# A tenth 2 MB place for experts' weights, a smaller ring for POOL's DMAs, three gather buffers instead of four

## What is computed

```python
def first_block(x, ...):
    h = rms_norm(x, norm_gain); proj = h @ w_in
    # attention over 31 compressed blocks, selected blocks and a window, all with
    # a shared bias by distance (rel_bias, 32 buckets); then the recurrence
    ...
    return x + m @ w_out

def second_block(x, ...):
    ...
    x = x + gate1 * (merged @ w_out)
    h2 = rmsnorm(x, norm2_w) * (1.0 + scale2) + shift2
    return x + gate2 * hierarchical_moe(h2, w_rg, b_rg, w_re, b_re, w_gate, w_up, w_down)

def hierarchical_moe(h, ...):       # top group, then 2 of its 8 experts for each token
    ...
    for e in range(N_EXPERTS):      # w_gate[e], w_up[e]: 1024 x 256, w_down[e]: 256 x 1024
        act = silu(hf @ w_gate[e]) * (hf @ w_up[e])
        y = y + combine[:, e:e + 1] * (act @ w_down[e])
```

## Time and profile before

| | |
|---|---|
| median of 3 runs | 1302.39 us (1296.23 to 1302.81) |
| the profiled execution, its own time | 1295.32 us |
| its span, first to last instruction | 1293.5 us |
| TensorE busy | 1220.6 us, 94% of the span |
| VectorE, ScalarE, POOL busy | 559.5, 307.6, 249.5 us |
| TensorE's mean granted clock | 0.983 of full speed |
| HBM read, written | 205.20 MB, 14.75 MB |
| share of the chain that ended last: TensorE, SP's queue, VectorE, DMA | 75%, 10%, 6%, 4% |

### The profile page before, as it was taken

The page is one execution under the profiler, slowest core; times in us unless marked ns, Lnnn a source line. Parts: engine busy times, 40 slices in busy tenths (PEclk is TensorE's granted clock), DMA queues, the critical chain, the costliest instruction groups (busy, mean ns, idle before and its releaser), DMA issues.

```text
span 1293.5 us, 13577 instructions
## 1 busy us (share of the span) xinstructions
PE 1220.6 (94%) x5056; PEld 692.7 (54%) x5056; DVE 559.5 (43%) x1432; ACT 307.6 (24%) x725; POOL 249.5 (19%) x221
## 2 busy tenths in 40 slices
PE   6999999999989999999999989999999999988885
PEld 3555444454544444488884445866674564433343
DVE  2214383477648751217992367522222442222221
ACT  4223644433310101124113245400000221111110
POOL 6100022354510000062420030302300021211100
PEclk9999999999999999999999999999999999998988
DMA  9625104223166514222223010302229489999995
GB/s 331 117 74 130 65 30 101 82 90 139 65 226 212 167 62 147 97 83 100 96 69 127 3 64 28 100 9 65 66 98 394 175 334 398 409 400 412 411 408 197
DMA packets 94935, 212.85 MB, mean 165 GB/s; under 512 B 20109, under 2 KB 54301, under 8 KB 83047
## 3 DMA queue, kind: packets, MB, share of 16 engines
q1 hardware_dynamic: 81344, 190.51, 39.8%
q0 software_dynamic: 10320, 18.80, 5.8%
q10 hardware_dynamic: 3200, 2.61, 0.6%
HBM read 205.20 MB, written 14.75 MB: 170 GB/s over the span
## 4 chain that ended last, share of the span: by engine, by line
PE 75%; SPq 10%; DVE 6%; DMA 4%; ACT 3%; issue 2%; ACTq 0%; POOL 0%; POOLq 0%; DVEq 0%
SPq L2825 8%; PE PS L2287 7%; PE PS L998 6%; PE PS L641 5%; PE PS L1415 4%; PE PS L2350 4%; PE PS L1495 4%; PE PS L1678 4%; PE PS L1680 4%; PE PS L2458 3%; PE PS L2957 3%; PE PS L1424 2%; PE PS L1724 2%; DMA AN<-in_w_down 2%; PE PS L1736 2%; PE PS L713 2%
## 5 line engine op out<-in xcount | busy, mean ns | idle before, releaser
L998 PE MATMUL PS<-HT,W 128*128 128x512 f32 x256 | 124.7, 610 | 1.8 <-ACT AN L1162 1.7
L1260 POOL TENSOR_SCALAR AN<-AN,SM 128x128 f32<-128x128 f32 (+3 forms) x64 | 72.5, 1140 | 197.2 <-DVE SM L1352 197.2
L1283 DVE SCALAR_TENSOR_TENSOR AN<-AN,COLA 128x256 f32<-128x256 f32 x168 | 85.9, 511 | 5.4 <-DMA AN<-in_w_ada 0.5
L2957 PE MATMUL PS<-AN,HT 128*64 128x512 f32 x192 | 61.6, 632 | 10.6 <-DMA X<-in_w_up 6.4
L641 PE MATMUL PS<-W,HT 128*128 128x512 f32 (+1 forms) x192 | 70.9, 531 | 0.0
L998 PEld LDWEIGHTS PS<-HT,W 128*128 128x128 f32 x256 | 44.4, 193 | 39.0 <-issue 35.4
L3042 DVE TENSOR_TENSOR HT<-HT,PS 128x256 f32<-128x256 f32 x16 | 6.7, 421 | 131.6 <-ACT HT L3017 131.6
L1415 PE MATMUL PS<-HT,W 128*128 128x512 f32 x128 | 58.1, 599 | 0.0
L2458 PE MATMUL PS<-W,AN 128*128 128x512 f32 x128 | 57.6, 597 | 0.0
L1242 ACT ACTIVATE AN<-PS,SM 128x128 f32<-128x128 f32 (+3 forms) x64 | 33.6, 525 | 93.9 <-DVE SM L1331 93.6
L2350 PE MATMUL PS<-AN,W 128*128 128x512 f32 x128 | 55.7, 593 | 0.1
(11 more groups left out here) (519 smaller groups left out, 2281.6 us busy)
## 6 DMA issues: line engine op xcount, KB each, us to landing
W<-in_w_in SPq DMA_DIRECT2D x14, 2048.0 KB, 9.0
W<-in_w_down SPq DMA_DIRECT2D x20, 1024.0 KB, 27.0
AN<-in_w_gate SPq DMA_DIRECT2D x17, 1024.0 KB, 26.9
AN<-in_w_up SPq DMA_DIRECT2D x17, 1024.0 KB, 28.8
AN<-in_w_ada SPq DMA_DIRECT2D x16, 1024.0 KB, 5.3
AN<-in_w_down SPq DMA_DIRECT2D x12, 1024.0 KB
W<-in_w_gate SPq DMA_DIRECT2D x10, 1024.0 KB, 24.4
W<-in_w_up SPq DMA_DIRECT2D x10, 1024.0 KB, 26.6
```

Source lines behind the costliest of these rows:

```text
L998: t = pe.matmul(u.ap, w[:, c, tile(m)], hT[:, c, :], start=c == 0, stop=c == 7)
L1260: pool.tensor_scalar(PU[u % 5][:, 0:n], PU[u % 5][:, 0:n], RSUM[:, u:u + 1], None, ALU.mult).then_inc(*sc_pool.up(u))
L1283: dve.scalar_tensor_tensor(out=a, in0=wt[:, c, :], scalar=ca["c2"][:, c:c + 1], in1=a, op0=ALU.mult, op1=ALU.add).then_inc(*ada_dve.up(p, c))
L2957: t = pe.matmul(u.ap[r, :].rearrange("p (n f) -> p n f", n=2), XGT[e % 2][:, c, r], w_gu(3 * e + half)[:, c], start=c == 0, stop=c == 7)
```

## The change

There are four parts. POOL's scratch of descriptors shrinks from 16384 to 4096 bytes a partition. The 12288 bytes (3072 numbers a partition) that this frees stand ahead of the area `AN`, and with the first 1024 numbers of `AN`, row 0 of `XN`, they make a tenth place. The gathers have three buffers, rows 3, 1 and 2 of `XN`, since row 0 is now part of that place. The four reads of `BCT` move from POOL's queue to SP's, with a semaphore of their own.

SP's order changes with it: the first half of load 9 goes out ahead of all other experts' loads and waits for nothing; the second half stands behind the second half of load 7 and waits for row 0 of `XN` to be written out and read by `pe_first_rows`. With NE = 10, it is loads 10 and 11 whose first halves wait for `first_pe`.

```diff
-    AN = sbuf("AN", AR)
+    ANX = sbuf("AN", 3072 + AR)
+    AN = ANX[:, 3072:3072 + AR]
...
-    XG = [XN[:, i, :] for i in range(4)]
+    XG = [XN[:, i, :] for i in (3, 1, 2)]
...
-    WE = [AN[:, a:a + 4096] for a in (6160, 10256, 18448)] + W[0:3] + [AN[:, 14352:18448], X, W[3]]
+    WE = [AN[:, a:a + 4096] for a in (6160, 10256, 18448)] + W[0:3] + [AN[:, 14352:18448], X, W[3], ANX[:, 0:4096]]
...
+    def sp_line(sp, ws):
+        ws.wait_ge(*line_out.at())
         for r in range(4):
-            pool.dma_start(BCT[31 * r:31 * r + 31],
-                           bass.AP(scr.tensor, 2048 * r, [[16, 31], [4 * 2048, 2], [1, 512]])).then_inc(*line_back.up())
+            sp.dma_start(BCT[31 * r:31 * r + 31],
+                         bass.AP(scr.tensor, 2048 * r, [[16, 31], [4 * 2048, 2], [1, 512]])).then_inc(*rows_back.up())
...
     def pe_bias(pe, wp):
...
             pe.matmul(u.ap, flip, REV[:, j * 512:(j + 1) * 512], start=True, stop=True).then_inc(*u.filled)
+        wp.wait_ge(*rows_back.at())
...
     def act_headnorm(act, wa):
...
+        wa.wait_ge(*rows_back.at())
...
-            act.dma_start(xnd[tile(i), :], XN[:, i, :]).then_inc(*xn_out.up())
+            act.dma_start(xnd[tile(i), :], XN[:, i, :]).then_inc(*xn_out[i].up())
...
     def wait_place(w, m, half=1):
...
-        else:
+        elif m == 8:
             w.wait_ge(*B.use("wo2", 3, 1).full)
+        elif half:
+            w.wait_ge(*xn_out[0].at())
+            w.wait_ge(*row_pe.at(0))
...
     def sp_expert(sp, ws, m, halves=(0, 1)):
         e, kind = divmod(m, 3)
         for n in halves:
-            wait_place(ws, m, n)
+            if m in (NE, NE + 1) and n == 0:
+                ws.wait_ge(*first_pe.at())
+            else:
+                wait_place(ws, m, n)
...
     def sp_expert_parted(sp, ws, e):
...
-                if m - NE in (0, 1) and n == 0:
-                    ws.wait_ge(*first_pe.at())
-                else:
-                    wait_place(ws, m)
+                wait_place(ws, m)
...
     def sp_experts(sp, ws):
+        sp_expert(sp, ws, 9, (0,))
         for m in range(6):
             sp_expert(sp, ws, m)
...
         sp_expert(sp, ws, 7, (1,))
-        for e in range(NE // 3, NP):
-            if e in (NE // 3, NP - 2, NP - 1):
+        sp_expert(sp, ws, 9, (1,))
+        for n in range(2):
+            sp_expert(sp, ws, 10, (n,))
+            sp_expert(sp, ws, 11, (n,))
+        for e in range(4, NP):
+            if e in (NP - 2, NP - 1):
...
     def pool_gather(pool, wg, e):
...
-        wg.wait_ge(*(row_pe.at(e) if e in (1, 2) else B.use("xg", max(e - 4, 0), 1).full))
+        wg.wait_ge(*(row_pe.at(e) if e in (1, 2) else B.use("xg", e - 3, 1).full))
         pool.indirect_dma_start(
-            out=XG[e % 4], ...
+            out=XG[e % 3], ...
...
     def sync_program(sp):
...
         sp_kvq(sp, ws)
+        sp_line(sp, ws)
         sp_cmp(sp, ws)
...
-    nc = _bacc.Bacc("TRN2", target_bir_lowering=False, num_devices=1)
+    nc = _bacc.Bacc("TRN2", target_bir_lowering=False, num_devices=1, dynamic_dma_scratch_size=4096)
```

More of the change, by code:

```diff
@@ L407, in build @@
         "consts_in", "gain_in", "line_in", "rows_in", "w2c_in", "small_in", "bd_in", "bars_in", "wr_in", "more_constants_in", step=16)
-    line_out, line_back, xn_out = sig("line_out", "line_back", "xn_out", step=16)
+    line_out, line_back, rows_back = sig("line_out", "line_back", "compressed_rows_back", step=16)
+    xn_out = sig(*[f"xn{i}_out" for i in range(NT)], step=16)
     x_spilled = sig(*[f"x{i}_spilled" for i in range(NT)], step=16)
@@ L418, in build @@
     stage_in = sig(*[f"stage{i}_in" for i in range(4)], step=16)
-    xg_in = sig(*[f"xg{i}_in" for i in range(4)], step=16)
+    xg_in = sig(*[f"xg{i}_in" for i in range(3)], step=16)
     yo_out = sig(*[f"yo{i}_out" for i in range(2)], step=16)
@@ L2884, in pool_gather @@
         wg.wait_ge(*(B.use("place2").out if e >= NP else B.use("place").out))
-        wg.wait_ge(*xn_out.at())
-        wg.wait_ge(*(row_pe.at(e) if e in (1, 2) else B.use("xg", max(e - 4, 0), 1).full))
+        for i in range(NT):
+            wg.wait_ge(*xn_out[i].at())
+        wg.wait_ge(*(row_pe.at(e) if e in (1, 2) else B.use("xg", e - 3, 1).full))
         pool.indirect_dma_start(
-            out=XG[e % 4], out_offset=None, in_=xnd, in_offset=bass.IndirectOffsetOnAxis(ap=TID[:, e:e + 1], axis=0),
-            bounds_check=S - 1, oob_is_err=False).then_inc(*xg_in[e % 4].up(e))
+            out=XG[e % 3], out_offset=None, in_=xnd, in_offset=bass.IndirectOffsetOnAxis(ap=TID[:, e:e + 1], axis=0),
+            bounds_check=S - 1, oob_is_err=False).then_inc(*xg_in[e % 3].up(e))
     def pool_scatter(pool, wg, e):
@@ L2915, in pe_turn_in @@
             wp.wait_ge(*u.free)
-            wp.wait_ge(*xg_in[e % 4].at(e))
+            wp.wait_ge(*xg_in[e % 3].at(e))
             for c4 in range(4):
-                t = pe.transpose(u.ap[:, tile(c4)], fv(XG[e % 4][:, 4 * q + c4:4 * q + c4 + 1], [[8, 128]]), ident)
+                t = pe.transpose(u.ap[:, tile(c4)], fv(XG[e % 3][:, 4 * q + c4:4 * q + c4 + 1], [[8, 128]]), ident)
             t.then_inc(*u.filled)
```

## The result

| | before | after |
|---|---|---|
| median of 13 runs, us | 1296.34 (1291.42 to 1302.81) | 1302.48 (1298.71 to 1309.21) |
| ratio of the times | | 1.0046, 95% interval 1.0028 to 1.0064 |
| profiled execution: time, span, us | 1295.32, 1293.5 | 1300.61, 1298.8 |

The forecast was 1300.8 us, made against a median of 1302.39 (three runs). Against the median of 13 runs, 1296.34, the same step of -1.6 us would have been 1294.7; what came was +6.0 (1296.34 x 0.0046). So the number was near by luck, and the sign was wrong.

A forecast was written before the change was run, and what follows sets the result against it. The prediction took bytes left to move after 1051 us at 398 GB/s to set the end. Its terms, -2.6 + 1.0 + 0 + 0 = -1.6 us, took 1302.39 to 1300.8 us; range 1294.5 to 1307.5.

The forecast's parts named there:

- What bounds the kernel: Experts' stage: bytes still to move after 1051 us, at 398 GB/s, set the end; TensorE sets the pace nearly everywhere before.
- The tenth place, first half: Load 9's first half lands in the half-idle DMA time before 1051 us, worth -2.6 us, nothing made late.
- Its second half: Load 9's second half, issued after 1051 us into a full queue, only changes its turn: 0 to 0.2 us, taken as 0.
- Three gather buffers: Gather e + 3 waits for tile e's transposes, rows needed three tiles later: cost 0, covered by some 30 us.
- Rival 3: Start of experts' stage gives back the first half's gain, such as gathers sharing with one more MB: 1302.4 us; chance 0.12.
- The smaller scratch: POOL's DMA issues: cost between 0 and some 5 us for waiting on one DMA in flight, taken as 0.
- Rival 4: POOL waits for scratch room with gathers and scatters in flight, only the last scatter open: up to +5 us; chance 0.06.
- The compressed lines on SP: Four BCT reads share one engine, semaphore at 61.0 us, TensorE wants them at 59.95: stall 1.0 us, bounds 0 to 9.3.
- 0.53 of their rate: BCT reads beside REV until 44.7 us: 0.53 x 11.7 = 6.2 us of their 21.7 us done by then.
- The upper bound: BCT reads with no overlap with REV: landing at 67.2 us, stall 7.3 us, plus 2 us for the clock's dip.
- rival 1: BCT reads pile up on one engine without overlapping REV, TensorE stalls: +6.7 us, 1309.1 us; chance 0.17.
- What stands behind them on SP: Compression weights behind BCT on SP land some 10 us later, hidden by over 25 us: no cost.

The follow-up runs named there:

- e4: e1 with load 9's second half behind loads 10 and 11 in SP's order; 1292.50 us, ratio 0.9952 to the kernel before.
- f2: e4 with both halves of load 9 behind loads 10 and 11, so no early first half; 1296.59 us, ratio 0.9994 to the kernel before.
- e1: The kernel after, with each BCT read of 31 rows cut into 16 and 15, still on SP; 1296.90 us, ratio 0.9994 to the kernel before.
- g3: The kernel before with three gather buffers and nothing else; 1297.26 us, ratio 0.9989.
- e2: The kernel before with only the four uncut BCT reads moved to SP; 1305.62 us, ratio 1.0061.
- g4: The kernel after, with REV read only once the four BCT reads have landed; 1312.87 us in one run, the reads landed by 56.5 us.
- f1: The kernel before with all of the change but the tenth place, BCT reads cut into 16 and 15 rows on SP; 1294.47 us, ratio 0.9974.
- e3: The kernel after, with the four BCT reads back on POOL, scratch of 4096 bytes; 1295.59 us, ratio 0.9994 to the kernel before.
- g1: The kernel before with a scratch of 4096 bytes and nothing else; 1303.81 us, ratio 1.0033.

## Why the prediction was wrong, step by step

- **What bounds the kernel.** Right for the end: the last load stands 28.84 us in a full queue, and the last landing sets the end. Incomplete: the stretch from 1051 to 1279 was read as one that is always full, with 29 us of slack for TensorE. It is full only if TensorE frees the places in time, and at the gather of tile 1 TensorE has no slack at all: it waits 0.96 us there even before.
- **The tenth place, first half: -2.6.** Sign right (e4 against f2, -0.42%, where -0.20% was forecast, at the edge of the intervals).
- **Its second half: 0.** Wrong by more than the gain of the first half. By e1 against e4 its turn costs 0.34%, some 4.4 us. It went ahead of loads 10 and 11, into the 7 to 9 us in which the gather of tile 1 runs. The step that failed is the sentence that this MB "only changes its turn", because the DMA engines would never be short of issued work; they were, at 309 GB/s from 1074 to 1084. Rival 3 had just this mechanism ("gathers at 1051 to 1057 that now share with one more MB") and I dismissed it by the 29 us of slack, an average over 228 us. That the gather's delay is the way in which it costs fits the table above and isn't proved by it; this stays open.
- **Three gather buffers: 0.** Right: 0.9989 (0.9968 to 1.0011). Gather 4 waits for the transposes of tile 1 and goes out at 1066.89, and nothing waits for it. The prediction's own sign of an error here, a gap in the share after 1055 or a late gather, did appear, and g3's profile has both; the median of g3 says that it isn't the buffers that cost.
- **The smaller scratch: 0, at most 5 on POOL.** Wrong on both sides. It gains 2.5 us at the end, and where POOL has five DMAs in flight it holds an issue for 10.9 or 16 us. In the kernel after the reads have left POOL and nothing is held. Rival 4 had the mechanism and the wrong place.
- **The compressed lines on SP: +1.0.** This is the term that turned the sign; it measured 6.4 us in the profile, and e2 alone makes 0.61%. One engine for all four was right (share 0.07), so the Trainium skill's rule (DMA: Bandwidth & Descriptors, "Why a DMA increments its semaphore by 16 and not by 1") is borne out, and e1 is its counter-test: by the rule 16 rows go to 16 engines and 15 rows to 15, and the wait was gone. The step that failed is "0.53 of their rate" while `REV` runs. It came from one window of 1 us with a share of 1.38, in which the projection weights and `REV` overlapped, and I carried it to another pair of transfers. From `REV`'s landing at 46.4 to 65.7 us, 19.3 x 25 = 483 of the 508 KB were moved, so only some 25 KB had gone before: about 2 GB/s on that engine and 0.08 of its rate, not 0.53. TensorE waited 4.5 us and not 1.0, and the fall of the clock, which the 1.0 leaves out, added the rest. The 0.8 us between the last byte and the semaphore in the sum has no row in any run; it is small beside the miss. The upper bound, 7.3 + 2 us, was right to have. The Trainium skill's rule that an engine takes packets from its queues in turn (same page, "Queues, rings and completion order") was on rival 1's side; whether such turns are the cause isn't shown here, only that with `REV` away the reads run at full rate (g4).
- **What stands behind them on SP.** Right: the compression weights took 19.3 us to land and not 8.1, and nobody waited.
- **Sum.** Forecast -2.6 + 1.0 = -1.6. Measured: reads +6.4, scratch -2.5 (both from profiles), tenth place as ordered about +2.6 (e1 against f1, 0.20%), buffers 0: +6.5, against +6.0 by the medians. That these meet so well is in part luck: the third term may be anything from -0.9 to +6.1, and the profile of the kernel after has +0.8 for that stage. What is firm is the first term, by the profiles (+6.4, and +6.6 in e2) and by the ratios (after against e1, 0.52%).

Rival 1 (+6.7, at 0.17) named the right cause, and by its own mark, a landing after 62.6 us, it is the case that came (65.7). Its total is near by luck as well: it reached it by 9.3 - 2.6; in truth it was 6.4 - 2.5 + about 2.6.

## What to carry to other kernels

Before a DMA is moved from one queue to another, count the DMA engines that its row count lets it use there, add up the bytes of all its sisters on that one engine, and assume next to no overlap on it with a slow transfer that keeps all engines busy. A full DMA queue is a bound only while the engine that frees its buffers keeps pace: look at the slack of the first waits of the stage, not at its mean, and try an extra load behind the small urgent transfers (here that turn gained 0.34%). An edit that is there to make room (a smaller scratch, another queue) has a price and a gain of its own; measure each alone.

## What the runs showed of the hardware

- A read of 31 rows on SP's queue used one DMA engine, and four of them the same one: share 0.07, 25 GB/s, 508 KB in 20.3 us; and the third issue held SP for 13.06 us. Cut in 16 and 15 rows they had landed before the product at 58.96.
- A transfer that keeps all engines at a share near 0.96 for only some 90 GB/s (`REV`) left to a second queue about 2 GB/s for each engine that it used (an estimate from 25 KB in 12 us on one engine, and from 122 against 90 GB/s over the same 12 us with the reads cut, e1); with `REV` away one engine had 26 GB/s (g4).
- After waits of TensorE of 3.8 and 4.5 us the granted clock was 0.57 over the next 8 and 4 us (kernel after), and the last product took 5.3 us at a granted clock of 0.53 to 0.66 and 3.67 at 1.00.
- The scratch's size shows in the end of the program: 8.0 to 8.4 us from the last issue to the end of the span at 16384 bytes, 7.4 at 8192, 5.5 to 6.0 at 4096.
- At 4096 bytes POOL had room for `REV` and three reads, and held the fourth for 10.9 us (e3) and 16.0 us (g1).
